# One core, hybrid decoder step: query weights fetched by whole rows with all query halves summed together, and the last work of a tile moved behind the next tile's first step

## What is computed

```python
q = (hb @ w_query).reshape(BLOCK, 8, 2, 128)          # 8 heads, 2 halves of 128
s = einsum('nhpd,hpkd->nhpk', q, sub_keys)            # 128 scores per head and half
s1, i1 = top_k(s[:, :, 0], 16); s2, i2 = top_k(s[:, :, 1], 16)
cand = s1[..., :, None] + s2[..., None, :]            # 256 candidates
top, sel = top_k(cand, 16); eidx = cidx[sel]; g = softmax(top)
act = gelu(einsum('nd,nhkd->nhk', hb, expert_u[eidx]))
out = einsum('nhk,nhkd->nd', g * act, expert_v[eidx]) # 128 experts per row
```

## Time and profile before

| what | value |
|---|---|
| median of 3 runs | 3812.92 us (3812.56 to 3818.82) |
| the profiled execution | 3811.95 us, its span 3810.0 us |
| PE, DVE, ACT, POOL busy | 81%, 65%, 41%, 33% of the span |
| DMA busy share by slice | 9 tenths or more in nearly all slices from 762 us on |
| bytes per second, same slices | 339 to 417 GB/s |
| expert gathers | 1,056 of 1 MB, median 14.5 us from issue to landing |
| loads of `w_query` | 72 of 1 MB, median 31 us to landing |

### The profile page before, as it was taken

The page is one execution under the profiler, slowest core; times in us unless marked ns, Lnnn a source line. Parts: engine busy times, 40 slices in busy tenths (PEclk is TensorE's granted clock), DMA queues, the critical chain, the costliest instruction groups (busy, mean ns, idle before and its releaser), DMA issues.

```text
span 3810.0 us, 44007 instructions
## 1 busy us (share of the span) xinstructions
PE 3081.3 (81%) x11576; PEld 1398.5 (37%) x11576; DVE 2461.8 (65%) x6391; ACT 1552.8 (41%) x4275; POOL 1267.0 (33%) x1139
## 2 busy tenths in 40 slices
PE   8999975578878886888788768887887788757887
PEld 2576632333433342334233423343343334312341
DVE  0232224588787587768766876687667766856785
ACT  0244311256345534542554345435543554334333
POOL 0000030134334433443434333434343334434443
PEclk9899986799999988998899889989998899889879
DMA  9511154589999999999999989999999999989998
GB/s 360 61 43 53 36 192 138 189 313 407 401 387 403 401 409 360 408 407 406 367 407 402 399 339 406 403 398 367 407 406 391 346 409 407 407 334 417 410 398 367
DMA packets 300854, 1291.72 MB, mean 339 GB/s; under 512 B 39382, under 2 KB 135526, under 8 KB 165284
## 3 DMA queue, kind: packets, MB, share of 16 engines
q0 software_dynamic: 156672, 1124.27, 73.5%
q1 hardware_dynamic: 143916, 164.51, 13.8%
HBM read 1271.34 MB, written 17.79 MB: 338 GB/s over the span
## 4 chain that ended last, share of the span: by engine, by line
DMA 28%; PE 22%; DVE 17%; issue 9%; ACT 6%; SPq 1%; POOL 0%; DVEq 0%; POOLq 0%; ACTq 0%
DMA ring<-experts_dram,idxc 28%; PE YY L1691 13%; DVE ring L1535 5%; PE M L1672 3%; PE TT L1678 3%; DVE yac L1282 2%; ACT gw L1249 1%; ACT dg L1257 1%; SPq L1041 1%; ACT L1247 1%; ACT ga L1247 1%; DVE eq L1338 1%; DVE eq L1341 1%; DVE sel L1343 1%; PE SS L1566 1%
## 5 line engine op out<-in xcount | busy, mean ns | idle before, releaser
L1691 PE MATMUL YY<-ring,dg 128*64 128x512 f32 (+1 forms) x4224 | 1802.4, 666 | 581.9 <-ACT dg L1257 561.1
L1128 POOL DMA_INDIRECT ring<-experts_dram,idxc x1056 | 1218.3, 1154 | 1830.1 <-PE YY L1691 1633.3
L1535 DVE CUSTOM_DVE_ANT_0 ring<-ring,h2c 128x1024 f32<-128x1024 f32 x1056 | 1271.7, 1225 | 594.1 <-DMA ring<-experts_dram,idxc 584.4
L1691 PEld LDWEIGHTS YY<-ring,dg 128*64 128x64 f32 (+1 forms) x4224 | 512.1, 147 | 1650.4 <-ACT dg L1257 920.1
L1247 ACT ACTIVATE ga<-act 128x1 f32<-128x1 f32 x1056 | 210.8, 200 | 968.9 <-DVE act L1535 965.9
L1257 ACT ACTIVATE dg<-fold,gw 128x64 f32<-128x64 f32 x1024 | 356.0, 348 | 50.7 <-ACT gw L1249 2.6
L1249 ACT ACTIVATE gw<-ga,gc 128x1 f32<-128x1 f32 x1056 | 311.0, 295 | 35.0 <-ACT ga L1247 1.0
L1282 DVE SCALAR_TENSOR_TENSOR yac<-win,cw,yac 128x128 f32<-128x128 f32 x960 | 262.7, 347 | 0.0
L1672 PEld LDWEIGHTS M<-fT,wq 128*128 128x128 f32 x1728 | 202.0, 196 | 49.7 <-issue 48.4
L1672 PE MATMUL M<-fT,wq 128*128 128x128 f32 (+1 forms) x1728 | 211.5, 282 | 0.4 <-DMA wq<-w_query_dram 0.4
L590 PE MATMUL A<-w_in,hT 128*128 128x512 f32 (+1 forms) x432 | 192.6, 606 | 5.4 <-ACT kTb L415 3.6
(11 more groups left out here) (304 smaller groups left out, 2514.4 us busy)
## 6 DMA issues: line engine op xcount, KB each, us to landing
wq<-w_query_dram SPq DMA_DIRECT2D x54, 1024.0 KB, 31.2
wa<-w_ada_dram SPq DMA_DIRECT2D x12, 2048.0 KB, 10.3
shared<-w_query_dram SPq DMA_DIRECT2D x18, 1024.0 KB, 31.8
ring<-experts_dram,idxc POOLq DMA_INDIRECT x1056, 14.5
w_in<-w_in_dram SPq DMA_DIRECT2D x8, 772.0 KB, 11.8
shared<-kT_scratch SPq DMA_DIRECT2D x16, 264.0 KB
w_in<-w_in_dram SPq DMA_DIRECT2D x1, 4096.0 KB, 20.6
xb<-x_prompt_dram SPq DMA_DIRECT2D x8, 512.0 KB, 5.4
```

Of the source, the lines that this page charges most:

```text
L1128: pool.indirect_dma_start(ring[:, k % RING, :], None, I["experts"], bass.IndirectOffsetOnAxis(idxc[:, k:k + 1], 0)).then_inc(g_in[k % RING ...
L1535: v.tensor_tensor_reduce(out=u, in0=u, in1=h2, scale=1.0, scalar=0.0, op0=ALU.mult, op1=ALU.add, accum_out=act8[:, k % RING:k % RING + 1]) ...
L1691: mm = pe.matmul(YY[o, half * 512:(half + 1) * 512], dg[:, k % DG, 0:w], ring[:, k % RING, D + half * 512:D + (half + 1) * 512], start=(k ...
```

## The change

- `wq` becomes 128 partitions of 2,048 numbers, and `load_wq(t, k)` loads the whole rows k*128 to k*128 + 127 of `w_query`: 1 MB in 128 runs of 8 KB. The waits for its three buffers keep their form.
- In steps S_ROUTE to S_ROUTE + 7 TensorE takes one such block each and adds its part to all 16 query halves at once (16 products of 128 x 128), which stand side by side in `SS` and `TT`. So no query is complete before the eighth block. `M0` is no longer used there.
- Heads follow from `S_HEAD` = S_ROUTE + 8: scores of head h at S_HEAD + 2h, `shortlist` at S_HEAD + 1 + 2h, `choose` at S_HEAD + 2 + 2h. The tile has 62 steps instead of 55. The 63 groups of the choice are spread as 2, 1 over the eight block steps (12), none at S_HEAD, 3 in each of 16 steps, then 2 and 1.
- The 64 products that turn `fT` back move to step S_HEAD + 15 (in tile 0 they stay first, and block 0 waits until ScalarE has copied their result out).
- VectorE's `end` becomes `finish`, and runs after step 0 of the next tile and its two groups. The copy of the gates moves from before step 0 to the first group of the tile. ScalarE's second step of a tile waits for `finish`, since it overwrites `PTs`.

```diff
-S_GATE = S_ROUTE + 4
+S_HEAD = S_ROUTE + DC
+S_GATE = S_HEAD + 3
...
-PLAN = ... + [4, 4] + [3, 3] * 7 + [4, 4] + [3, 2]
+PLAN = ... + [2, 1] * 4 + [0] + [3] * 16 + [2, 1]
...
-                sp.dma_start(wq[b][:, :, :], wqv[:, :, h * 2 * NK:(h + 1) * 2 * NK]).then_inc(wq_in[b], 16)
+                sp.dma_start(wq[b][:, :], I["w_query"][h * P:(h + 1) * P, :]).then_inc(wq_in[b], 16)
...
+                        if s == 1 and some(t) and not (isinstance(t, int) and t == 1):
+                            act.wait_ge(y_ready, t - 1)
...
+                    act.wait_ge(qd_done, DC * (t + 1))
+                    if some(t) or h:
+                        act.wait_ge(sc_done, H * t + h)
+                    made = (SS, TT)[h // 4][:, h % 4 * 2 * P:(h % 4 + 1) * 2 * P].rearrange("p (g t) -> p g t", g=2)
...
-                if s == S_ROUTE:
+                if s == (S_HEAD + 2 * H - 1 if some(t) else S_ROUTE):
                     pe.wait_ge(fT_ready, t + 1)
+                    if some(t):
+                        pe.wait_ge(qh_ready, H * t + H)
...
+                if S_ROUTE <= s < S_ROUTE + DC:
+                    k = s - S_ROUTE
+                    b = k % 3
+                    if k == 0:
+                        pe.wait_ge(fT_ready, t + 1)
+                        if not some(t):
+                            pe.wait_ge(cur_ready, FOLD)
+                    pe.wait_ge(wq_in[b], 16 * ((2 if b == 2 else 3) * t + k // 3 + 1))
+                    for i in range(2 * H):
+                        mm = pe.matmul((SS, TT)[i // H][:, i % H * P:i % H * P + r], wq[b][:, i * NK:(i + 1) * NK], fT[:, k, 0:r],
+                                       start=(k == 0 and i % 4 == 0), stop=(k == DC - 1), skip_group_check=True)
                     mm.then_inc(qd_done, 1)
...
             def group(e, k):
                 u = ring[:, k % RING, 0:D]
-                if not some(e) and k == 0:
-                    v.wait_ge(cur_ready, FOLD)
+                if k == 0:
+                    if some(e):
+                        take_gates(e)
+                    else:
+                        v.wait_ge(cur_ready, FOLD)
...
             step(s, t, nk)
             for k in range(upto[s], upto[s + 1]):
                 group(t - 1, done + k)
+            if s == 0 and not (isinstance(t, int) and t == 1):
+                finish(t - 2)
         end(t - 1)
```

More of the change, by code:

```diff
@@ L895 @@
 S_KEEP = 6
-PLAN = [2, 2, 2, 3] * 4 + [2, 1, 1, 1, 2, 2, 1, 1, 2, 2, 2, 2] + [2, 1, 1, 1, 1, 2, 2] + [4, 4] + [3, 3] * 7 + [4, 4] + [3, 2]
+PLAN = [2, 2, 2, 3] * 4 + [2, 1, 1, 1, 2, 2, 1, 1, 2, 2, 2, 2] + [2, 1, 1, 1, 1, 2, 2] + [2, 1] * 4 + [0] + [3] * 16 + [2, 1]
 PLAN_0 = [0] * (S_GATE + 1) + [2] * 12 + [3] * 3
@@ L922, in tail @@
         shared = sb("shared", [P, 2 * SEQ])
-        wq = [sb(f"wq{i}", [P, DC, 2 * NK]) for i in range(2)] + [shared[:, :].rearrange("p (k n) -> p k n", k=DC)]
+        wq = [sb(f"wq{i}", [P, 2 * H * NK]) for i in range(2)] + [shared]
         subk = sb("subk", [P, H, 2, NK])
@@ L1193, in step @@
                     a.then_inc(fT_ready, 1)
-                if s == S_ROUTE + 1:
+                if s == S_ROUTE:
                     if not some(t):
                         fold_h2(0)
[L1198 to L1201, removed]
+                if S_HEAD <= s + 1 < S_HEAD + 2 * H and (s + 1 - S_HEAD) % 2 == 0:
+                    h = (s + 1 - S_HEAD) // 2
+                    act.wait_ge(qd_done, DC * (t + 1))
+                    if some(t) or h:
+                        act.wait_ge(sc_done, H * t + h)
+                    made = (SS, TT)[h // 4][:, h % 4 * 2 * P:(h % 4 + 1) * 2 * P].rearrange("p (g t) -> p g t", g=2)
                     if smp:
@@ L1208, in step @@
                         act.activation(qh[:, :, :], made, ACT.Copy).then_inc(qh_ready, 1)
-                if S_ROUTE <= s < S_ROUTE + 2 * H and (s - S_ROUTE) % 2:
-                    h = (s - S_ROUTE) // 2
+                if S_HEAD <= s < S_HEAD + 2 * H and (s - S_HEAD) % 2 == 0:
+                    h = (s - S_HEAD) // 2
                     act.wait_ge(sc_done, H * t + h + 1)
@@ L1477, in step @@
                     modulate(r)
-                if S_ROUTE + 2 <= s < S_ROUTE + 2 + 2 * H:
-                    (choose if (s - S_ROUTE) % 2 else shortlist)(t, (s - S_ROUTE - 2) // 2)
-                if s == S_ROUTE + 1 + 2 * H and some(t):
+                if S_HEAD + 1 <= s < S_HEAD + 1 + 2 * H:
+                    (shortlist if (s - S_HEAD) % 2 else choose)(t, (s - S_HEAD - 1) // 2)
+                if s == S_HEAD + 2 * H and some(t):
                     write_indices(t)
@@ L1511, in keep_x1, with take_gates @@
                 v.tensor_copy(yb[0:r, :], xb[0:r, :]).then_inc(x1_kept, 1)
-            def begin(e):
-                if not some(e):
-                    return
+            def take_gates(e):
                 flat = gn[:, :, :].rearrange("p h k -> p (h k)")
+                v.wait_ge(gelu_done, 2 * NG * e)
                 if isinstance(e, int) and e == NB:
@@ L1536, in group, with finish @@
                                        op1=ALU.add, accum_out=act8[:, k % RING:k % RING + 1]).then_inc(dot_done, 1)
-            def end(e):
+            def finish(e):
                 r = height(e)
@@ L1555, in prologue @@
                 v.wait_ge(cst, 4)
-            iterate(v, step, group, begin, end, prologue)
+            iterate(v, step, group, lambda e: None, lambda e: None, prologue, finish)
         @block.tensor
@@ L1707, in keys_of, with iterate @@
     return P if t == 0 else SEQ // 2 if t < NB // 2 else 3 * SEQ // 4 if t < 3 * NB // 4 else SEQ
-def iterate(eng, step, group, begin, end, prologue):
+def iterate(eng, step, group, begin, end, prologue, finish=lambda e: None):
     def both(t, nk, done=0):
@@ L1735, in iterate @@
         group(NB, k)
+        if k == 0:
+            finish(NB - 1)
     end(NB)
+    finish(NB)
 def build(nc, I, O, S):
```

1 line of the change is left out of this document (removed).

## The result

The changed kernel took 3914.5 us, median of 4 runs (3903.2 to 3921.6), against 3815.3 for the kernel before beside it: ratio 1.0261, interval 1.0245 to 1.0277. Forecast: 3898, 3865 to 3945 for the likeliest case. The profiled run took 3912.45 (span 3910.5), 100.5 more than the profiled run of before.

What follows compares the result with a forecast made beforehand. DMA engines were taken to set the pace, VectorE close behind. Terms -9 + 39 + 27 + 20 + 8 = +85 us on 3811.95 gave 3897, median 3898; likeliest case 3865 to 3945 (0.62), whole range 3840 to 3960.

Steps and rivals of the forecast that it cites:

- Bound before: In the choice of experts DMA engines set the pace (share 1.00); VectorE, with few microseconds to give per tile, comes next.
- Loads: Whole-row loads gain 1.3 us per tile beside attention, -9 over tiles 1 to 7; nothing in the choice.
- Queries together: Choice, tiles 1 to 8: first scores 48.3 us after first block, VectorE idles 34.5; less idle before, +39.
- Tile 0: First tile, no groups to cover: first MAX8 28 us later, 1 or 2 us come back, +27.
- New waits: Choice of experts: engines near their limit wait for each other, 2.5 us in each of 8 tiles, +20 (ends 0, 48).
- The blocks' loads: Block steps of the choice: TensorE's blocks do not wait for loads, 0 taken; upper end +9 in 8 tiles, 72.
- rival B: Block steps of the choice: blocks starve for loads, +72 on the sum, 3970 us; chance 0.12.
- End of a tile: Turn to the next tile: later y delays first sums 1.5 us in tiles 2 to 7, 1.3 taken, +8.
- The hole that POOL might have closed: Loop turn: POOL gets indices earlier, so part of a 4 us hole in DMA share may close; VectorE doesn't wait for it.
- A: Transfers stay the only bound: tiles 1 to 8 gain, -60, only tile 0 loses, 3779 us; chance 0.08.
- C: Ring's eight slots and slack in attention take up the choice's losses; only first two tiles lose, 3853 us; chance 0.15.
- The signs: What would show the forecast in the profile: MAX8 times, VectorE's waits, DMA share, load landing times, first sums, tile 1 most lengthened.

Runs made afterwards that it cites:

- b_pack: Kernel before, heads still one by one, with only w_query laid out so each head's load is 128 runs of 8 KB: 3787.3 us, ratio 0.9936.
- a_wide8: Changed kernel with tile 8's blocks 128 columns wide instead of 32: 3882.2 us, ratio 1.0173 to the kernel before.
- a_end: Changed kernel with y made at the end of its own tile again, as before the change: 3902.8 us, ratio 1.0241 to the kernel before.
- a_1k: Changed kernel with each block loaded as two DMAs of 512 runs of 1 KB: 4011.6 us, ratio 1.0515 to the kernel before.
- b_finish: Kernel before with only the end of a tile moved (y after the next tile's first step, gates' copy with the first product): 3820.6 us, ratio 1.0021.

## Why the prediction was right, and where it was off

**Bound before.** Right as a picture (transfers first, VectorE close behind), too firm on VectorE: in the choice after the change the DMA share is still 1.00, and VectorE is busy 91% of the time behind its first scores, so the two are nearly level.

**Loads.** The packets' gain was forecast at 3.5 us per tile and b_pack shows 3.2 on average. I let only the 1.3 beside attention count, as VectorE was to pace the choice. The choice of tile 3 seems to fall from 185.3 us to 181.6, but 3.0 of this is the wait for the last sums, which lies outside the later window. With equal ends it is 182.3 to 181.6. How much of the other 2.2 arrived in the changed kernel is not shown.

**Queries together.** Block to MAX8 was forecast at 48.3 (tile 1: 44.3) and came at 46.4 (44.3). Block 7 of tile 3 ended 43.2 us after the first block began, where I had 45.6. Most of this is the price of a group. I took 1.36, a third of three in a row, but one group alone takes as long as two in a row:

```profile
1743.05 1.94 PE L1701 MATMUL YY<-ring,dg 128*64 128x512 f32 x8
1748.69 1.93 PE L1701 MATMUL YY<-ring,dg 128*64 128x512 f32 x4
```

So the seven stretches of 2, 1, 2, 1 groups took 13.1 us and not 14.9, and in tile 1, with more groups alone, nothing was gained. MAX8 came 3.1 us behind the blocks where I had 2.7. VectorE's idle time in the choice changed as the account said: +26.0 in tile 1 (10.8 to 36.8; forecast +23), -0.2 in tile 3 (forecast -1), -0.8 in tile 6, +5.9 in tile 7 (+7.6). But it is not one wait for scores. The prediction said that a wait for scores under 25 us would make it wrong at its main step, and in tiles 1 to 7 that wait is 4.3 to 17.7. What stands is that the scores come 46 us after the first block, with 12 products to do until then; what fell is that VectorE would do these products at once and then stand. Their gathers came late, beside the burst of loads. Tile 8 was off: +34.7 for +9.5. The step that failed there is "its blocks load the same weights, so 3.84 taken too"; at the lower clock a block takes 7.0 and the groups between them twice as long, and a_wide8 gives back 26.8.

**Tile 0.** +27 forecast, +29.6 in the profile, +23.2 in those of a_end and a_wide8. The wait for the copies to h2c is as forecast: block 0 starts 2.1 us behind the products to row form in every profile with blocks. The spread is in part TensorE's clock. These products and the first block took 6.7 and 5.3 us in the changed kernel's profile, at granted clocks of 0.55 and 0.59, and 5.0 and 3.6 in that of a_end, at 0.73 and 1.00. The first half of that block in a_end, against the 3.09 at 708.95:

```profile
704.47 2.02 PE L1678 MATMUL SS<-fT,wq 128*128 128x128 f32 x16 [2.09 <-issue]
```

The other 3 us are an earlier start of the whole stretch in a_end.

**New waits.** 20 us taken over eight tiles, the weakest term. Tiles 2 to 6 came out at -4.2 where the terms said +11.5, while tile 1 took 6.2 more than its sum. On the profiled run tiles 1 to 8 come to +68.2, less 26.8 for the clock in tile 8, so 41; the forecast for them was 58 with the 20 and 38 without. The 20 stood where about 4 belonged, and this hid that tile 8's clock was missing from the sum: the sum is only 15 us short of the measured 100.5 because -16 in tiles 2 to 6 stands against the clock's 25. That part of the right total is luck.

**The blocks' loads.** Taken at 0, and TensorE did not wait for them (2.1 us, put down to issue). The time of a load was near, 8.9 us forecast and 9.6 measured, but by luck: the ratio of 2.5 gathers per packet from the y rows is a misreading. Its window of 8.6 us holds 3.4 us in which no packet of y ran yet. In 1496 to 1499 the count is 109 packets of q1 to 116 of q0, one for one. So it is in the blocks; the queues in 1747 to 1751, during a load:

```profile
q1 hardware_dynamic: 106, 0.87, 51.7%
q0 software_dynamic: 114, 0.81, 48.9%
```

A load begins 3.4 us after its issue (issued at 1743.1, no packet of q1 before 1746.6) and then holds half of the DMA time for about 5 us (an estimate: 8 rows per engine, each with one of the gathers beside it, at the 0.32 us per 8 KB of the earlier trace rows). That is under the 5.6 us in which TensorE asks for the next, while 9.6 is not, because 9.6 contains the 3.4 at the start. This is why rival B fails for rows of 8 KB. With rows of 1 KB blocks do wait, and a_1k shows it at 97 us. The Trainium skill, "DMA: Bandwidth & Descriptors", "Queues, rings and completion order", has a DMA engine drain a whole packet of several descriptors at its turn. A load's eight rows per engine are not such a packet by the trace: rows of the two queues went one for one.

**End of a tile.** 1.3 us in each of six tiles forecast, +8; b_finish measured +8 (0.21%, interval 0.12% on either side) and a_end -8 by its ratio (0.20%, 0.18% on either side of each of the two ratios). The hole that POOL might have closed was not measured by itself.

**Rivals.** A fails at the point where it was to decide, MAX8 within 40 us of the block. C is nearer the truth of tiles 2 to 6 than my own term: they absorb the change. What it lacked is tiles 7 and 8, +42 together, 27 of it the clock.

**The signs.** Those that came: tile 0's MAX8 and first indices, the landing of the loads, no wait of TensorE for them, the first sums at 13.5. Those that did not: one wait for scores of 34 us, a DMA share under 0.97 (0.99 to 1.01), and tile 1 as the most lengthened (30.4, tile 8 31.9).

**Left open.** Why blocks of 32 columns got the lower clock: that it goes when the same blocks are 128 columns wide is shown, not how. In tile 8 the blocks 1 to 3 ran at 7.0 us and blocks 4 to 7 at 3.9 to 4.4, at 1.00 inside block 4, with the groups between those still at 3.1 to 3.6, at 0.50 behind block 4: that order is not explained. Nor is the 4 us per tile by which tiles 2 to 7 in blocks stay behind b_pack.

## What to carry to other kernels

Split a change into its parts before it is judged: here the load's layout alone gives 0.6% and the reordering that came with it takes three. Work moved ahead of the first result of a stretch costs nothing only as long as the engine behind it had as much idle time there, so do the account per tile: the first two of a pipeline had none here. Work gathered into one stretch also gathers its loads, and they take DMA time from whatever else feeds that stretch. And where a remainder uses narrower operands, price it by a row of that width in that order, not by the wide one.

## What the runs showed of the hardware

A block of sixteen fp32 products of 32 columns took 7.0 us at a granted clock of 0.50, and 3.8 with 128 columns at 1.00, both with TensorE busy without a gap. Padding was the faster form. At a clock of 1.00 the width did not matter: sixteen products of 32 columns in a row took 3.76 us in the kernel before, of 128 columns 3.84.

Two queues that both had work went nearly packet for packet, whatever the size: 1,680 of 1 KB to 1,680 of the gathers, 109 of the y store (4 KB) to 116, 106 of a load's rows (8 KB) to 114. So a load of 1 MB beside the gathers landed in 31.2 us as 1 KB runs and in 9.4 as 8 KB runs (b_pack, same order of work), at a share of the DMA time only 0.9 points lower: here the run's length decides the latency far more than the throughput. Of such a load 3.4 us pass before its first row.
